# Product-key expert layers: whole tables as dense products with a gate matrix, in place of row gathers

## The reference, cut to what matters

```python
q = (xb @ w_query).reshape(tb, PEER_HEADS, 2, PEER_KEY_DIM // 2)
s = jnp.einsum('thpd,pnd->thpn', q, sub_keys)
top_s, top_i = lax.top_k(s, k)                     # 16 of 128, for each of two halves
cand_s = top_s[:, :, 0, :, None] + top_s[:, :, 1, None, :]
cand_i = top_i[:, :, 0, :, None] * PEER_N_KEYS + top_i[:, :, 1, None, :]
best_s, best_j = lax.top_k(cand_s.reshape(tb, PEER_HEADS, k * k), k)
idx = jnp.take_along_axis(cand_i.reshape(tb, PEER_HEADS, k * k), best_j, axis=-1)
gate = jax.nn.softmax(best_s, axis=-1)
u = expert_u[idx]
act = jax.nn.gelu(jnp.einsum('thkd,td->thk', u, xb))
w = (gate * act)
return jnp.einsum('thk,thkd->td', w, expert_v[idx])
```

## Time and profile before

| | us |
|---|---|
| median of 3 runs | 2175.0 |
| the three runs | 2160.2, 2175.0, 2183.93 |
| span of the profiled execution, first to last instruction | 1970.9 |
| median minus span | 204.1 |

### The profile page before, as it was taken

One profiled execution on the slowest core, in us unless ns is written; L12 is line 12 of the kernel. 1 busy time (PEld: TensorE's weight loads), 2 busy tenths in 40 slices (PEclk: granted clock), 3 DMA queues, 4 the chain that ended last, 5 costly groups with the idle time before them and its releaser, 6 DMA issues.

```text
span 1970.9 us, 17348 instructions
## 1 busy us (share of the span) xinstructions
PE 1577.1 (80%) x4322; PEld 776.4 (39%) x4322; DVE 1155.1 (59%) x2896; ACT 301.0 (15%) x950; POOL 1046.2 (53%) x1143
## 2 busy tenths in 40 slices
PE   8999979896666666999989968977999666666666
PEld 3467636352222222444434524433445322222222
DVE  2433236665666667666677666655676666666661
ACT  1033112121111111321111211200111111111111
POOL 1110026666666666566656656656565665666662
PEclk9955599997878788999989979988999988888887
DMA  5210118998999899999999999999999999999985
GB/s 175 87 44 11 74 69 323 403 351 332 346 337 340 335 349 336 347 389 397 395 370 375 405 379 359 377 404 350 361 360 400 360 355 337 338 346 335 342 334 191
DMA packets 184121, 616.73 MB, mean 313 GB/s; under 512 B 19275, under 2 KB 20811, under 8 KB 184054
## 3 DMA queue, kind: packets, MB, share of 16 engines
q0 software_dynamic: 152064, 553.72, 74.3%
q1 hardware_dynamic: 31990, 62.23, 8.6%
HBM read 614.83 MB, written 1.05 MB: 312 GB/s over the span
## 4 chain that ended last, share of the span: by engine, by line
PE 53%; issue 16%; POOL 10%; DVE 10%; DMA 8%; ACT 1%; POOLq 0%; DVEq 0%; SPq 0%; ACTq 0%
PE bank L816 23%; PE bank L616 12%; POOL arena L556 10%; DVE arena L1445 8%; DMA arena<-peer_u,idx_now 8%; PE bank L804 4%; PE bank L717 3%; PE bank L802 2%; PE bank L932 1%; PE bank L689 1%; PE bank L678 1%; DVE h L1472 1%; PE bank L780 1%; PE bank L605 1%; PE bank L766 1%
## 5 line engine op out<-in xcount | busy, mean ns | idle before, releaser
L816 PE MATMUL bank<-arena 128*128 128x512 f32 x2112 | 925.8, 598 | 21.0 <-ACT arena L1077 19.7
L1445 DVE CUSTOM_DVE_ANT_0 arena<-arena,bank 128x1024 f32<-128x1024 f32 x528 | 628.9, 1219 | 478.3 <-DMA arena<-peer_u,idx_now 468.8
L556 POOL DMA_INDIRECT arena<-peer_v,idx_now x528 | 511.2, 968 | 434.1 <-PE bank L816 331.6
L816 PEld LDWEIGHTS bank<-arena 128*128 128x128 f32 x2112 | 405.7, 193 | 548.0 <-issue 547.8
L556 POOL DMA_INDIRECT arena<-peer_u,idx_now x528 | 499.2, 945 | 196.8 <-issue 135.5
L802 PE MATMUL bank<-skT,q_now 128*128 128x256 f32 x66 | 34.0, 612 | 331.0 <-DVE dots L1445 274.9
L616 PE MATMUL bank<-wring,hT 128*128 128x512 f32 (+5 forms) x604 | 260.8, 589 | 2.5 <-ACT hT L973 1.6
L616 PEld LDWEIGHTS bank<-wring,hT 128*128 128x128 f32 (+1 forms) x604 | 108.5, 182 | 145.5 <-issue 139.8
L1077 ACT ACTIVATE arena<-con,wgt 128x128 f32<-128x128 f32 (+1 forms) x528 | 157.8, 387 | 31.6 <-DVEq L1468 31.6
L802 PEld LDWEIGHTS bank<-skT,q_now 128*128 128x128 f32 x66 | 14.4, 271 | 351.6 <-issue 351.6
L1071 ACT ACTIVATE gl<-gl 128x16 f32<-128x16 f32 x33 | 7.1, 215 | 786.2 <-DVEq L1460 786.2
(11 more groups left out here) (158 smaller groups left out, 1045.8 us busy)
## 6 DMA issues: line engine op xcount, KB each, us to landing
wring<-gla_w_in SPq DMA_DIRECT2D x12, 2048.0 KB, 19.8
arena<-peer_u,idx_now POOLq DMA_INDIRECT x528, 6.6
arena<-peer_v,idx_now POOLq DMA_INDIRECT x528, 6.8
wring<-gla_w_out SPq DMA_DIRECT2D x4, 2048.0 KB, 19.6
wring<-peer_w_query SPq DMA_DIRECT2D x4, 2048.0 KB, 23.0
wring<-attn_w_in SPq DMA_DIRECT2D x2, 2048.0 KB, 8.3
wring<-attn_w_out SPq DMA_DIRECT2D x2, 2048.0 KB, 7.8
gws<-peer_w_query SPq DMA_DIRECT2D x2, 2048.0 KB, 10.4
```

The costliest lines, as they stand in the source:

```text
L556: nc.gpsimd.indirect_dma_start(out=rows[:, k % RING, :], out_offset=None, in_=table.rearrange("l e d -> (l e) d"), in_offset=bass.Indirect ...
L816: last = nc.tensor.matmul(yacc[:, 512 * i:512 * i + 512], wplace[:, k, :], vrow[:, k % RING, 512 * i:512 * i + 512], start=(k == 0), stop= ...
L1445: v.tensor_tensor_reduce(out=urow[:, k % RING, :], in0=urow[:, k % RING, :], in1=xrep, scale=1.0, scalar=0.0, op0=ALU.mult, op1=ALU.add, a ...
```

## The change

Both expert layers are computed for the 256 tokens at once, from the whole tables. No row of them is gathered for these tokens. A tile is 128 rows of a table (512 KB), 128 tiles for each table of a layer; tile i holds the experts whose first key is i.

- First stage, over the tiles of u: TensorE turns the tile (8 transposes of 128x128), ScalarE copies it out of PSUM (`firstT`, two buffers), TensorE multiplies it with `hT` of 256 tokens (8 products of 128x128 with 128x256), and ScalarE's gelu writes the result to `slab` in SBUF (128 experts of the tile, 128 tiles, 256 tokens), two tiles in one instruction.
- Gate matrix: the picks of a token are turned so that they lie on 128 partitions. For each token, GpSimd makes a matrix of its gates placed by second key (128x128), VectorE one that places by first key (128x64, half the first keys), and TensorE multiplies the two: 64 groups of 8 tokens and half the keys in each layer. VectorE multiplies `slab` by the result. The 32 groups of the first half stand behind tiles 65, 67, ... 127 of the first stage, those of the second half among the first 56 tiles of the second stage.
- Second stage, over the tiles of v: 4 products of 128x128 (a block of tokens of `slab`) with 128x512, added up in four PSUM banks over all 128 tiles.
- Tiles come in by 256 plain DMAs of SyncE in each layer, through 5 slots.
- The meta tokens of layer 0 are still gathered (16 and 16 indirect DMAs), with their dot products on VectorE and their mix on TensorE behind tile 54.
- The choosing is done for 128 tokens at a time, head by head, with the decoding moved to GpSimd.
- With no groups to lie between, the attention outputs, the queries, and the GLA mixer now stand in a row: attention, queries, experts, GLA for all blocks at once (its weights read once, through four slots), queries, experts.

```diff
-            def gathers(g, par, layer, side=None, side_at=("v", 11)):
...
+            def load_tile(layer, n):
+
+                before = n - STREAM
+                if 0 <= before < TILES:
+                    sp.wait_ge(t_filled, TILES * layer + before + 1)
+                elif before >= TILES:
+                    sp.wait_ge(second_used, TILES * layer + before - TILES + 1)
...
+                sp.dma_start(stream[s], table[layer, P * (n % TILES):P * (n % TILES) + P, :]).then_inc(tile_in[s], 16)
...
+            def decode(layer, b):
+
+                pool.wait_ge(chosen, 2 * layer + b + 1)
+                for s in range(2):
+                    for a in range(TOPK):
+                        steps.did(nc.gpsimd.tensor_scalar(onehot[:, a, :], digit_f[b][:, s, :], float(a), None, ALU.is_equal))
...
+                    for w in (8, 4, 2):
+                        steps.chain(nc.gpsimd.tensor_tensor(onehot[:, 0:w, :], onehot[:, 0:w, :], onehot[:, w:2 * w, :], ALU.add))
...
+            def spread_second_keys(layer, half, r):
...
+                for t in range(GROUP):
+                    n = GROUP * r + t
+                    nc.gpsimd.tensor_scalar(a_ring[:, g % 2, t, :], const("iota"), turned[:, 1, n:n + 1], turned[:, 2, n:n + 1],
+                                            ALU.is_equal, ALU.mult).then_inc(a_ready, 1)
...
-            def mix(g):
...
+            def turn_tile(layer, i):
+
+                n = TILES * layer + i
+                s, loads = stream_slot(layer, i)
+                pe.wait_ge(tile_in[s], 16 * loads)
+                at_least(pe, t_taken, n - 1)
+                for c in range(KC):
+                    last = nc.tensor.transpose(bk(2 * (i % 2), P * c, P * c + P), stream[s][:, P * c:P * c + P], ident)
+                last.then_inc(t_filled, 1)
+
+            def multiply_tile(layer, i):
+
+                n = TILES * layer + i
+                pe.wait_ge(t_taken, n + 1)
+                at_least(pe, gelu_done, n // 2 - 1)
+                a = (4 + (i // 2) % 2) * 512 + T * (i % 2)
+                for c in range(KC):
+                    last = nc.tensor.matmul(bank[:, a:a + T], firstT[i % 2][:, c, :], hT[:, c, P:P + T], start=(c == 0), stop=(c == KC - 1))
+                last.then_inc(y_filled, 1)
...
+            def gate_matrix(layer, half, r):
+
+                g = (2 * layer + half) * GROUPS + r
+                pe.wait_ge(a_ready, GROUP * (g + 1))
+                pe.wait_ge(b_ready, g + 1)
+                at_least(pe, g_taken, g - 1)
+                to = bk(6 + g % 2).rearrange("p (k t) -> p t k", t=GROUP)
+                for t in range(GROUP):
+                    last = nc.tensor.matmul(to[:, t, :], a_ring[:, g % 2, t, :], b_ring[:, g % 2, t, :], start=True, stop=True)
+                last.then_inc(g_filled, 1)
...
+            def mix_tile(layer, i):
...
+                for b in range(2):
+                    for x in range(2):
+                        last = nc.tensor.matmul(bk(2 * b + x), slab[:, i, P * b:P * b + P], stream[s][:, 512 * x:512 * x + 512],
+                                                start=(i == 0), stop=(i == TILES - 1))
+                last.then_inc(second_used, 1)
...
+            def take_turned(layer, i):
...
+                nc.scalar.activation(firstT[i % 2].rearrange("p c e -> p (c e)"), bank[:, 1024 * (i % 2):1024 * (i % 2) + 1024],
+                                     ACT.Copy).then_inc(t_taken, 1)
...
+            def gate_slab(layer, half, r):
...
+                v.tensor_tensor(part_of, part_of, bk(6 + g % 2).rearrange("p (k t) -> p k t", t=GROUP), ALU.mult).then_inc(g_taken, 1)
```

More of the change, by code:

```diff
@@ new lines, in build @@
+        cand, cand_rest, rest = part(big, 34816, 256), part(big, 35072, 256), part(big, 35328, 2, N_KEYS)
+        onehot = part(big, 32768, TOPK, P)
+        den = small[:, 32:40]
+        turned = part(picks, 0, 3, T)
+        q_meta = part(picks, 0, P)
+        score_meta = part(picks, P, 2 * N_KEYS)
+        meta = sb("meta", [P, 336])
+        take = taker(meta, 0, 336)
+        m_top, m_top_i, m_top_f = take(2, TOPK), take(2, TOPK).bitcast(U32), take(2, TOPK)
+        m_best, m_best_j = take(TOPK), take(TOPK).bitcast(U32)
@@ new lines, in build @@
+        gv = take(NB, GVD)
+        gr = take(2, GVD)
+        la = take(NB, GKD)
+        ex = take(NB, GKD)
+        qdT = take(2, GKD)
+        kdT = take(2, GKD)
+        state = [take(GH, GV) for _ in range(4)]
+        og = take(2, GVD)
+        g1T = take(NB, P)
+        g1 = take(NB, RANK)
+        dec = take(2, 2 * GH)
+        gms = take(2, 8)
+        kd = [la[:, b, :] for b in FULL]
+        atm = [ex[:, i, :] for i in range(2)]
+        sq = [gq.rearrange("p b n -> p (b n)"), la[:, 1:3, :].rearrange("p b n -> p (b n)")]
@@ L584, in _ @@
+            for b in FULL:
+                root(small[:, b:b + 1], small[:, 3 + b:4 + b], 1)
         @block.tensor
@@ L1188, in _ @@
+            meta_queries()
+            queries(0)
+            experts(0)
+            take_gains(2)
+            mixer()
+            queries(1)
+            experts(1)
+            take_gains(4)
         @block.vector
@@ L1210, in roots, with norm_sums @@
                 dve.wait_ge(norm_rs, n_norm[0])
-            def norm(n, blocks):
+            def norm_sums(blocks):
                 for b in blocks:
@@ new lines, in experts @@
+            def experts(layer):
+                if layer == 0:
+                    choose_meta()
+                choose(layer, 0)
+                if layer == 0:
+                    dot_meta()
+                gates(layer, 0)
+                choose(layer, 1)
+                gates(layer, 1)
+                if layer == 0:
+                    dve.wait_ge(m_mixed, TOPK)
+                    v.tensor_tensor(h[:, 0, :], h[:, 0, :], y_meta, ALU.add).then_inc(m_added, 1)
+                order = [(half, r) for half in range(2) for r in range(GROUPS)]
+                spread_first_keys(layer, *order[0])
+                for n, (half, r) in enumerate(order):
+                    if n + 1 < len(order):
+                        spread_first_keys(layer, *order[n + 1])
+                    gate_slab(layer, half, r)
+                if layer == 0:
+                    dve.wait_ge(m_added, 1)
+                    norm_sums([0])
+                    roots()
+                dve.wait_ge(second_used, TILES * (layer + 1))
+                for b in FULL:
+                    v.tensor_tensor(h[:, b, :], h[:, b, :], bank[:, 1024 * (b - 1):1024 * b], ALU.add).then_inc(acc_taken, 1)
```

1405 lines of the change are left out of this document (724 added, 681 removed).

## The result

| | forecast | measured |
|---|---|---|
| time of the changed kernel, us | 3095 (3015 to 3300) | 2849.0, four runs from 2846.9 to 2852.0 |
| before, timed beside it, us | 2175.0 | 2174.1, four runs from 2160.2 to 2183.9 |
| ratio | 1.42 | 1.311, 95% interval 1.305 to 1.317 |
| span of the profiled execution, us | 2892 | 2847.1 |
| time less span, us | 204.1 | 1.9 |

The last two rows say where: the span was met within 1.6%, and what was to lie around it isn't there. The profiled execution took 2848.94 us, of which the profile shows 2847.1.

What follows compares the result with a forecast made beforehand. TensorE was taken to bound the kernel, with 53% of the chain. The span summed 339 + (1129 + 28) + 250 + 1129 + 17 = 2892 us; 204.1 around it, carried over, gave 3095 us, range 3015 to 3300.

Steps and rivals of the forecast that it cites:

- I carry these over unchanged: 3096: Around the span: the 204.1 us by which before's median exceeds its profiled span is added to 2892, giving 3096.
- The rival in which that part grows: Around the span: what lies there grows with the span, giving 3192 us; chance 0.12.
- The start at 339 us: Before the expert layers: turning, output products, meta queries, queries and scores end so that the experts start at 339 us.
- the copies and gelus beside the products: First stage: ScalarE's copy and half a gelu, 1.34 us in a tile of 4.4, hide beside TensorE's products.
- the loads hidden at 512 KB each: Expert stages: SyncE's tile loads, 2.8 us alone or 5.0 beside gathers, are taken as hidden behind TensorE.
- the clock of 1.00 in the new stages: Expert stages: they are dense, so counted at 2.4 GHz, with a granted clock near 1.0.
- 128 x (0.96 + 3.44 + 3.44): Expert layer, 128 tiles: transposes 0.96, first-stage products 3.44 and second-stage products 3.44 us a tile, 1003 us a layer.
- 64 x 1.9 us for the gate groups: Gate matrix on TensorE: 64 groups a layer of 16 records, 1.9 us each, 123 us a layer.
- GLA and queries 250, tail 17: Between the expert layers GLA, queries and open waits take 250 us; after the last product the end takes 17.
- its rival: Gate groups: GpSimd at 1.34 us an operation sets the second stage's pace, 90 us a layer more, 3275 us; chance 0.07.
- The rule that speaks otherwise: Dense products: the skill's 131 ns for sustained 512-column pairs, 0.61 of the price used, would give about 2409 us; chance 0.02.
- the first stage and the gate matrix, forecast at 686 us a layer: Expert layers: new TensorE work of 563 + 123 us a layer, against 462 us regained in both layers together.

Runs made afterwards that it cites:

- a_gate1: The changed kernel with one product in place of eight in each gate group (output not the reference's): 2653.6 us.
- bfloat16 kernel: The changed kernel with both dense products in bfloat16, gate groups reordered and half the second-key spreading on VectorE: 1629.9 us, ratio to before 0.827; again on a slow chip 1622.5, 0.739.
- a_turn1: The changed kernel with one transpose in place of eight in each first-stage tile after the first two (output not the reference's): 2655.5 us.

## Why the prediction was right and wrong, point by point

- **"I carry these over unchanged: 3096".** This is the step that failed. The 204.1 us "around the span" were taken as a property of the program, from one profile's span and three other times. They measure 1.8 to 2.1 us in every execution of every run. The span's own sum with 1.9 us behind it is 2894, 1.6% over the measured 2849. The result lies in the range without them (3015 - 204 = 2811 at its lower end). The rival in which that part grows (3192, chance 0.12) fails with it. I had written that the profile gives no time of its own for that part; a gap of 10% that no view shows should have been a doubt with a chance of its own, and the case "nothing lies around the span" at 2892 was missing among the rivals.
- **The start at 339 us** was met (339.1). So were the copies and gelus beside the products, the loads hidden at 512 KB each, and the clock of 1.00 in the new stages.
- **128 x (0.96 + 3.44 + 3.44).** The products were right, 3.45 and 0.429 x 8 = 3.43. The transposes were 0.88, not 0.96: 2 x 128 x 0.08 = 20 us in both layers. Part of that lies in the reading of the earlier trace rows: 2.00 us for 16 go to the end of the last one, and the next work starts before that end. Here eight take 1.04 us to the end and 0.88 to the next start.
- **64 x 1.9 us for the gate groups.** The records of 64 columns cost 0.109 by a_gate1, not 0.12, so 1.74 a group: 20 us in both layers. These two terms give 40 of the 45 us by which the span was over: experts 1138 and 1106 against 1157 and 1129.
- **GLA and queries 250, tail 17**: 249 and 15.1.
- **GpSimd** was mis-sized, 0.817 us an operation where I took 0.3, though within the bounds up to 1.34 that I had kept; the condition for its rival, more than 7.9 us a group, was not met.
- **The rule that speaks otherwise** falls. The row is 0.429 us for a record of two passes, 0.215 a pass, in a stage of 1024 such records with a new weight load before each. The bfloat16 kernel shows a pass alone: eight records of 256 columns in 0.88 us, 0.110 each, in a stage where TensorE is busy 315.55 of 340 us. At 512 columns it has only bursts of four: records of 0.383 us mean length (its group of L962) end 1.04 us after the first starts, so about (1.04 - 0.383) / 3 = 0.219 us from one to the next, an estimate, since the ends of records are modelled. The Trainium skill, "TensorE: Matmul & The Clock Gate", section "Back-to-back issue gap", gives 131 ns for sustained pairs and calls 216 the isolated gap; here the sustained pairs run at the 216.
- **Slower in total, and why**: the first stage and the gate matrix, forecast at 686 us a layer, came to 128 x (0.88 + 3.45) + 64 x 1.74 = 666 by the measured prices. For 2 x 666 = 1332 us the kernel got back 462, the pauses (331.0 us in all) and the small products of the groups. That is 870 us more, and the spans differ by 2847.1 - 1970.9 = 876. That the DMA engines now move 137 and 120 GB/s in the expert stretches, where the kernel before had 346 in its last 440 us of expert groups, saves nothing where TensorE is the bound. The ratio hangs on the chip through the kernel before: 2846 / 2188 = 1.30 on one of the slow kind, while 2849 over the 1966 of the first chip would be 1.45, an estimate, as the changed kernel wasn't timed there. The forecast ratio of 1.42 lies near that by luck: its time was too high by 9%, and so was its divisor for such a chip, by 11%.

## What to carry to other kernels

A time and a span that don't belong to the same execution are two measurements: before their difference becomes a term of a sum, ask for a run that shows both, and give "there is no such part" a chance. Count a dense replacement by its records first: with TensorE 98% busy, each float32 record here was paid in full, one after the other. The dense form puts 128 times as many rows before each token, and in this kernel that paid only with a type that makes a record cheap (3.45 us a tile against 0.88). And measure a kernel with many row gathers on more than one chip before its ratio to a kernel without them is trusted.

## What was unexpected of the hardware

- The kernel with 1056 row gathers takes 1966 to 1968 us on two of the chips and 2188 to 2202 on two others (2174 where it was first timed), while the same kernel with plain DMAs takes 1927 to 1934 on three chips of both kinds, the changed kernel 2846 on a slow one (2849 when first timed), and the bfloat16 kernel 1630 and 1623.
- On the slow chips idle gaps of 1.2 to 2.5 us stand between short instructions of VectorE and TensorE in the kernel that gathers, while the instructions themselves are as long as elsewhere. In its expert groups there are also longer ones, up to 22.2 us before a mix (L816).
- A GpSimd comparison and multiplication of 128x128 with two scalars for each partition takes 817 ns, a comparison alone with a constant 568 ns; VectorE does the first in 358 ns, and 278 ns apart (from the group of those operations in the bfloat16 kernel).
- A transpose of 128 columns and a record of a float32 product of 64 columns cost the same, 0.109 us by a_turn1 and a_gate1, where a float32 record of 256 columns costs 0.216.
